# Expert weights in two transfers of 4 MB and two of 2 MB, with 32 KB and 16 KB of each partition in one run

## The reference

```python
h = h + mixed @ w_out[l]
h = h + moe(rms_norm(h, ffn_norm_w[l]), ...)
# moe:
logits = xt @ router_w + router_b
top_val, top_idx = lax.top_k(logits, 4)
gates = softmax(top_val)
# for each expert, on the tokens that chose it:
gu = xb @ w_gate_up[e] + b_gate_up[e]          # 1024 -> 2048
g, u = minimum(gu[:, :1024], 7), clip(gu[:, 1024:], -7, 7)
act = (u + 1) * (g * sigmoid(1.702 * g))
y = (act @ w_down[e] + b_down[e]) * gate       # 1024 -> 1024
```

## Time and profile before

| | |
|---|---|
| median of 3 runs | 1201.25 us (1198.61 to 1202.64) |
| profiled execution, first to last instruction (its span) | 1198.2 us; no other time of it was taken |
| TensorE busy | 1138.6 us (95%) |
| VectorE, ScalarE, GpSimd busy | 258.0, 172.6, 7.3 us |
| moved by DMA | 431.91 MB, mean 360 GB/s |
| gate/up loads | 256 of 1 MB, median 19.3 us from issue to landing |
| down loads | 128 of 1 MB, median 14.0 us |
| granted TensorE clock | 0.994 of full speed |

### The profile page before, as it was taken

How to read it: one execution, slowest core, us unless ns; L and a number is a source line. 1 busy time by engine, 2 the same in 40 slices (tenths; PEclk the granted TensorE clock), 3 DMA queues, 4 the chain that set the end, 5 groups by cost and what they waited for, 6 DMA issues and landing times.

```text
span 1198.2 us, 16109 instructions
## 1 busy us (share of the span) xinstructions
PE 1138.6 (95%) x6363; PEld 572.3 (48%) x6363; DVE 258.0 (22%) x657; ACT 172.6 (14%) x337; POOL 7.3 (1%) x16
## 2 busy tenths in 40 slices
PE   4999999799999999999999999999999999999997
PEld 3777776444444444444444444444444444444442
DVE  2487762631111111111111111111111111111101
ACT  2443240411000000000110000000000000000000
POOL 1000000000000000000000000000000000000000
PEclk9999999989999999999999999999999999999999
DMA  9953247699999959999999999999999999999995
GB/s 251 243 176 105 106 156 287 242 353 383 394 419 417 418 219 410 418 418 417 418 418 418 417 418 418 418 418 418 417 418 417 419 417 418 417 418 418 418 418 234
DMA packets 106452, 431.91 MB, mean 360 GB/s; under 512 B 9251, under 2 KB 37102, under 8 KB 73630
## 3 DMA queue, kind: packets, MB, share of 16 engines
q1 hardware_dynamic: 106206, 431.19, 90.8%
q0 software_dynamic: 224, 0.43, 0.1%
HBM read 430.54 MB, written 1.05 MB: 360 GB/s over the span
## 4 chain that ended last, share of the span: by engine, by line
PE 84%; DMA 7%; SPq 4%; ACT 3%; issue 1%; DVE 1%; DVEq 0%; ACTq 0%
PE psum L763 31%; PE psum L783 17%; PE psum L792 9%; DMA arena<-in_w_gate_up 6%; PE psum L566 5%; PE psum L750 4%; PE psum L732 4%; PE psum L486 4%; SPq L343 3%; PE psum L624 2%; PE psum L661 2%; ACT arena L999 1%; PE psum L592 1%; PE psum L742 1%; ACT arena L991 1%
## 5 line engine op out<-in xcount | busy, mean ns | idle before, releaser
L763 PE MATMUL psum<-arena 128*64 128x512 f32 x2048 | 448.4, 593 | 4.3 <-DMA arena<-in_w_gate_up 3.7
L763 PEld LDWEIGHTS psum<-arena 128*64 128x64 f32 x2048 | 192.2, 137 | 253.4 <-issue 240.0
L783 PE MATMUL psum<-arena 128*64 128x512 f32 x1024 | 228.3, 598 | 25.5 <-ACT arena L999 25.5
L1287 DVE TENSOR_SCALAR arena<-psum 128x512 f32<-128x512 f32 x32 | 22.1, 691 | 795.8 <-PE psum L763 784.0
L783 PEld LDWEIGHTS psum<-arena 128*64 128x64 f32 x1024 | 73.3, 138 | 159.9 <-issue 158.0
L792 PE MATMUL psum<-arena 128*128 128x512 f32 x256 | 117.8, 602 | 0.7 <-ACT arena L1003 0.7
L987 ACT COPY arena<-psum 128x512 f32<-128x512 f32 x32 | 18.7, 585 | 503.4 <-PE psum L732 503.4
L792 PEld LDWEIGHTS psum<-arena 128*128 128x128 f32 x256 | 45.8, 189 | 48.6 <-issue 47.0
L732 PEld LDWEIGHTS psum<-arena 128*128 128x128 bf16 x1536 | 48.4, 98 | 29.1 <-issue 29.1
L750 PE MATMUL psum<-arena 128*64 128x512 f32 x256 | 62.0, 598 | 0.0
L566 PE MATMUL psum<-arena 128*128 128x256 f32 x256 | 61.7, 385 | 0.3 <-ACT arena L924 0.3
(11 more groups left out here) (210 smaller groups left out, 540.6 us busy)
## 6 DMA issues: line engine op xcount, KB each, us to landing
arena<-in_w_gate_up SPq DMA_DIRECT2D x256, 1024.0 KB, 19.3
arena<-in_w_down SPq DMA_DIRECT2D x128, 1024.0 KB, 14.0
arena<-in_w_in SPq DMA_DIRECT2D x27, 512.0 KB, 6.7
arena<-in_w_out SPq DMA_DIRECT2D x1, 4096.0 KB, 16.8
arena<-in_w_o_mla SPq DMA_DIRECT2D x1, 2048.0 KB, 9.8
arena<-in_conv_pw_w SPq DMA_DIRECT2D x1, 2048.0 KB, 15.0
arena<-in_x SPq DMA_DIRECT2D x3, 512.0 KB, 6.5
out_y<-arena SPq DMA_DIRECT2D x4, 256.0 KB, 2.4
```

Of the source, the lines that this page charges most:

```text
L763: last = mm(b[64 * half:64 * half + 64, :], xe[i][:, k, :], gu[i][k][:, o + half * 512:o + half * 512 + 512], start=(k == 0 and bias_last) ...
L783: last = mm(Y[64 * c:64 * c + 64, :], aT[:, k % 4, 64 * (k // 4):64 * (k // 4) + 64], dn[i][:, u, c * 512:(c + 1) * 512], start=(k == 0), ...
```

## The change

- A gate/up load becomes two transfers of 4 MB. Partition p of half c gets rows 4p to 4p+3 of the half's 512 rows: 32 KB in one run. A down load becomes two of 2 MB, 16 KB a partition. There is one semaphore a transfer, and `gu_done` and `dn_done` count two an expert.
- As the rows of a weight block now belong to other partitions, the gathered state is stored in the matching order (`row_order`), and `turn_act` transposes every fourth column.
- `scatter` reads 64 partitions instead of 128; `wp` and `sT` shrink to two tiles, so `turn` has two transposes instead of four. The biases are kept at partitions 0 to 31 (gate) and 32 to 63 (up), and `pick` has 32 rows for each.
- The order of issue changes at EARLY = 20 instead of 6. The last expert's second down half is loaded in four pieces of 512 KB.
- Ahead of the items gu(0) waits for the ring as a whole, and gu(1) is loaded in two halves, after `h1_ready` and after `split_ready`.
- Clears of `biasgu` and `wp` on GpSimd go.

```diff
+GC, GR = 2, 4
+DC, DR = 2, 4
...
-        gu = [[words((A0, B0)[i] + 2048 * k, 2048) for k in range(KD)] for i in range(2)]
-        dn = [grid(D0 + 2048 * i, 2, 1024) for i in range(4)]
+        gu = [[grid((A0, B0)[i] + 8192 * c, GR, 2 * FF) for c in range(GC)] for i in range(2)]
+        dn = [grid(D0 + 4096 * h, DR, D) for h in range(DC)]
...
+        def row_order(y):
+            return y.rearrange("p (c q j) -> p c j q", c=GC, j=GR)
...
-                    src = weights_gu[e, k * P:(k + 1) * P, :]
...
-                sp.dma_start(gu[i][k], src).then_inc(in_gu[i][k], 16)
+                src = src[:, c * GR * P:(c + 1) * GR * P, :].rearrange("a (p j) f -> p (a j) f", j=GR)
+                sp.dma_start(gu[i][c], src).then_inc(in_gu[i][c], 16)
...
-                src = src[:, 2 * i * P:(2 * i + 2) * P, :].rearrange("a (k p) c -> p (a k) c", p=P)
-                sp.dma_start(dn[i], src).then_inc(in_dn[i], 16)
+                src = src[:, h * DR * P:(h + 1) * DR * P, :].rearrange("a (p j) f -> p (a j) f", j=DR)
+                sp.dma_start(dn[h], src).then_inc(in_dn[h], 16)
+
+            def load_last():
+                src = weights_dn[E - 1, DR * P:2 * DR * P, :].rearrange("(p j) f -> p j f", j=DR)
+                for j in range(DR):
+                    sp.dma_start(dn[1][:, j, :], src[:, j, :]).then_inc(in_last[j], 16)
...
-            for k in range(2, 6):
-                sp.wait_ge(*piece_used["g", k])
-                load_gu(0, 0, k)
+            sp.wait_ge(*piece_used["g", 7])
+            load_gu(0, 0, 0)
...
-            for k in (0, 1, 6, 7):
-                load_gu(0, 0, k)
+            load_gu(0, 0, 1)
             sp.wait_ge(S.mix_ready, 4)
...
+            sp.wait_ge(S.h1_ready, 4)
+            load_gu(1, 1, 1)
+            sp.wait_ge(S.hT_ready, 4)
             sp.wait_ge(S.xn_ready, 2)
+            sp.wait_ge(S.logits_ready, 2)
+            sp.wait_ge(S.split_ready, 2)
             load_gu(1, 1, 0)
...
-                for k in range(KD):
-                    sp.wait_ge(S.gu_done, 8 * (n - 2) + (k + 1))
-                    load_gu(n, u, k)
+                for c in range(GC):
+                    sp.wait_ge(S.gu_done, GC * (n - 2) + (c + 1))
+                    load_gu(n, u, c)
...
-                for i in range(4):
-                    sp.wait_ge(S.dn_done, 4 * (n - 1) + (i + 1))
-                    load_dn(n, i)
+                for h in range(DC):
+                    sp.wait_ge(S.dn_done, DC * (n - 1) + (h + 1))
+                    load_dn(n, h)
...
-            EARLY = 6
+            EARLY = 20
...
+            next_gu(E - 2, 0)
+            next_dn(E - 2)
+            next_gu(E - 1, 1)
+            sp.wait_ge(S.dn_done, DC * (E - 2) + 1)
+            load_dn(E - 1, 0)
+            sp.wait_ge(S.dn_done, DC * (E - 1))
+            load_last()
...
-                for c in range(2):
-                    for t in range(2):
-                        j = 2 * c + t
-                        last = nc.tensor.transpose(X[:, j * P:(j + 1) * P], wp[i][:, t, 64 - 64 * c:192 - 64 * c],
-                                                   ident)
+                for t in range(2):
+                    last = nc.tensor.transpose(X[:, t * P:(t + 1) * P], wp[i][:, t, :], ident)
...
-                        last = mm(b[64 * half:64 * half + 64, :], pick[i],
-                                  biasgu[:, o + half * 512:o + half * 512 + 512], start=first, stop=not first)
+                        last = mm(b[64 * half:64 * half + 64, :], pick[i][E * o:E * (o + 1), :],
+                                  biasgu[E * o:E * (o + 1), half * 512:half * 512 + 512], start=first, stop=not first)
...
-                        last = mm(total(t, c), sT[i][:, 2 * c + t, :], y_s, start=False, stop=False,
-                                  skip_group_check=True)
+                        last = mm(total(t, c), sT[i][64 * c:64 * c + 64, t, :], y_s[64 * c:64 * c + 64, :],
+                                  start=False, stop=False, skip_group_check=True)
...
-                for c in range(4):
-                    last = nc.tensor.transpose(Y[:, c * P:(c + 1) * P], a_s[:, c * P:(c + 1) * P], ident)
+                cols_of = a_s.rearrange("p (q j) -> p j q", j=DR)
+                for j in range(DR):
+                    last = nc.tensor.transpose(Y[:, j * P:(j + 1) * P], cols_of[:, j, :], ident)
```

More of the change, by code:

```diff
@@ L216, in layer @@
         xe = [grid(at + 1024 * i, KD, SLOTS) for i in range(2)]
-        sT = [grid(at + 1024 * i + 512, 4, P) for i in range(2)]
+        sT = [grid(at + 1024 * i + 512, 2, P) for i in range(2)]
         bdown = words(at + 1024, D); at += 2048
@@ L397, in _ @@
             next_dn(EARLY + 1)
-            with sp.Fori(0, (E - EARLY - 2) // 2) as it:
+            with sp.Fori(0, (E - EARLY - 4) // 2) as it:
                 for u in range(2):
@@ L407, in _ @@
                     e = sp.value_load(ove[0:1, bass.ds(j, 1)], min_val=0, max_val=E - 1)
[L408 to L413, removed]
+                    sp.wait_ge(S.gu_done, GC * j + GC * E)
+                    for c in range(GC):
+                        load_gu(e, 0, c)
+                    sp.wait_ge(S.dn_done, DC * j + DC * E)
+                    for h in range(DC):
+                        load_dn(e, h)
             for i in range(4):
@@ L758, in gate_up @@
                 pe.wait_ge(S.xe_ready, n + 1)
-                for k in range(KD):
-                    pe.wait_ge(in_gu[i][k], loads)
-                    for o, b in ((0, G), (FF, U)):
-                        for half in range(2):
-                            last = mm(b[64 * half:64 * half + 64, :], xe[i][:, k, :],
-                                      gu[i][k][:, o + half * 512:o + half * 512 + 512],
-                                      start=(k == 0 and bias_last), stop=(k == KD - 1 and not bias_last))
-                    if k == KD - 1 and bias_last:
+                for c in range(GC):
+                    pe.wait_ge(in_gu[i][c], loads)
+                    for j in range(GR):
+                        k = GR * c + j
+                        for o, b in ((0, G), (FF, U)):
+                            for half in range(2):
+                                last = mm(b[64 * half:64 * half + 64, :], xe[i][:, k, :],
+                                          gu[i][c][:, j, o + half * 512:o + half * 512 + 512],
+                                          start=(k == 0 and bias_last), stop=(k == KD - 1 and not bias_last))
+                    if c == GC - 1 and bias_last:
                         last = biases(i, False)
@@ L804, in item @@
                 turn_act(n)
-                down(n, dn_loads)
+                down(n, (dn_loads, dn_loads), in_pieces=final)
             free(6)
@@ L822, in _ @@
             turn_act(0)
-            down(0, 16)
+            down(0, (16, 16))
             gather(1, 1)
```

96 lines of the change are left out of this document (45 added, 51 removed).

## The result

The changed kernel takes 1171.9 us (median of 4 runs, 1167.8 to 1172.9). The kernel before, run beside it, takes 1201.5. The ratio is 0.975 (0.973 to 0.977), so 29.6 us are gone. The forecast was 1167, its range 1157 to 1194. The profiled execution took 1171.8 with a span of 1170.0, against a forecast span of 1163.6. The span is 6.4 us over its forecast and the time only 4.9: an execution takes 1.6 to 1.8 us more than its span, and the forecast had added 3.05.

What follows compares the result with a forecast made beforehand. The DMA weight stream was taken as the bound. Last landing: run length -26, switch -12, slower start +2, old hitches -2; the end gives back 4. Span 1163.6 plus 3.05 gave 1167 us, range 1157 to 1194.

Steps and rivals of the forecast that it cites:

- Runs: Weight stream: 96 fewer runs an engine and expert save 0.89 us, from 30.14 to 29.25 us an expert.
- B: Rival for the weight stream: it gets no faster, 30.14 us an expert, time 1193 us; chance 0.15.
- D: Rival for the weight stream: long runs read slower, kernel slower beyond 30.43 us an expert; chance 0.09.
- E: Rival: the same time, with a mildly slowed stream of 30.3 to 30.55 us an expert; chance 0.05.
- Scatter: TensorE's scatter in each item: from 3.52 to 1.76 us, perhaps 0.4 more, bounds 1.76 and 3.52.
- Biases: TensorE's biases in each item: unchanged at 1.72 us with 32 rows, lower bound below 0.9.
- The start of the stream: First loads: gu(3) issued at 285.1 flows from 287.4, 5 us unused; slower start +2 us.
- the permuted copies: Reordered copies of the state: cost nothing, as they lie beside the DMA bound.
- The gap at the switch: Change of issue order at dn(21): 0.8 us of transfer time unused instead of 13.0.
- The end: After gu(31) lands at 1136.5: 6.9 + 4.9 + 7.1 + 8.2 us to the span's end at 1163.6.
- the switch's 12 us: Moving the change of issue order from dn(7) to dn(21): -12 us of the last landing.

Runs made afterwards that it cites:

- the full scatter: Changed kernel with scatter over 128 rows and four transposes in turn again, biases still at 32 rows: 1177.74 us, ratio 0.9819.
- TensorE's part alone: Kernel before with scatter over 64 rows, two transposes in turn and biases with 32 rows; loads and order of issue unchanged: 1185.45 us, ratio 0.9872.
- run length alone undone: Changed kernel with each partition's rows 128 apart again, so runs of 8 KB (gate/up) and 4 KB (down), same transfers: 1195.55 us, ratio 0.9957.
- the half load ahead: Changed kernel with one half of gu(22) issued ahead of dn(21), the other behind its first half: 1169.01 us, ratio 0.9734.
- the finest version: Changed kernel with half of gu(22) ahead of dn(21), and gu(2), gu(3) first halves and gu(31) second half in 1 MB transfers: 1164.7 us, ratio 0.9697.

## Why the prediction was right, and what it missed

The mechanism held: the stream bounds the kernel, longer runs quicken it, and TensorE has to be out of its way. The profiled span came 6.4 us over the forecast, by terms that were mis-sized at the start and at the switch. Point by point:

**Runs: right, with some luck.** 29.25 us forecast, 29.22 measured. The rows were read as 7.5 to 9 ns a run, and the sum took 0.89 us, which is 9.3 ns a run, because eight completions would go as well. The completions cost nothing and a run costs 9.4 ns: two errors that cancel. With 7.5 ns the forecast would have been 29.42 us an expert and 5 us more in all. Rivals B (no faster), D (long runs slower) and E fall with this row. The pitch between partitions is the length of a run in each of the three layouts, so the two weren't tried apart; as all three lie on one line in the number of runs, a pitch of 32 KB did no harm that shows. The packets are 3,300 fewer than forecast because the small ones were not counted.

**Scatter: right.** 1.76 to 2.2 us forecast, 1.92 measured. By the Trainium skill ("TensorE: Matmul & The Clock Gate", Part 3) matmuls in different row groups run together; the trace agrees, 3.52 to 1.92 with the same eight instructions. Each of them takes as long as before, 615 ns in the mean against 602, but the two of a pair, one in the upper and one in the lower rows, start within 10 ns of each other. The end of the turn was then not late any more for the activation, as forecast.

**Biases: missed.** They stand at 1.72 in the sum, with the lower bound at 0.9; measured 1.02. The same mechanism as for scatter was assumed there and not carried over to here. So the item is 27.04 and not 27.8 us. It made no difference to the end, as the DMA was the bound either way, but the waits came at item 7 or 8 instead of about 10. Even with the full scatter it kept the item below the DMA's 29.2.

**The start of the stream: mis-sized, +3.7 us.** The forecast has gu(3) flowing from 287.4. Of the changed kernel, the first items of TensorE, then the issue of gu(3):

```profile
246.51 14.89 PE L772 MATMUL psum<-arena 128*64 128x512 f32 x64 [0.55 <-ACT arena L1029]
...
268.95 8.75 PE L795 MATMUL psum<-arena 128*64 128x512 f32 x32 [0.67 <-ACT arena L1013]
...
281.29 13.95 PE L772 MATMUL psum<-arena 128*64 128x512 f32 x64
```

```profile
L350 SPq DMA_DIRECT2D arena<-in_w_gate_up x1: 333/333/333, 288.6 to 288.6; - x1
...
DMA to landing us min/median/max: 12.2/12.2/12.2
```

It was issued at 288.6 and landed at 300.8. Its 4 MB take 9.72 at full rate, so it flowed from 291.1. The forecast built on TensorE's times of the earlier trace rows, and gate_up(0) began 3.06 us later. 1.8 of these are in the trace from the first matmuls on, which the change doesn't touch: 0.4 in 24 matmuls near 15 us (4.17 and 4.58 us) and most of the rest in the 96 behind them, first in the kernel before, then in the changed one:

```profile
19.84 22.16 PE L486 MATMUL psum<-arena 128*128 128x272 f32 x96 [0.39 <-DVE arena L1071]
```

```profile
20.16 23.62 PE L496 MATMUL psum<-arena 128*128 128x272 f32 x96 [0.38 <-DVE arena L1085]
```

The full clock was granted from 18.7 us in the one execution and from 23.2 in the other. In the profiles of the eight experiments it came between 18.8 and 19.5 or between 23.2 and 24.4 us, with no relation to their edits. A term read from a single profile carries this.

The other 1.3 us belong to the change. The forecast put the permuted copies at nothing, as lying beside the DMA bound. But the loads from gu(2) on wait for TensorE's first items, and these wait for the copies: a cast on ScalarE and a subtraction on VectorE stand ahead of the first gather (last line of each group); the kernel before, then the changed one:

```profile
233.11 1.04 ACT L974 CAST arena<-arena 128x1024 bf16<-128x1024 f32 x1 [1.55 <-DVE arena L1239]
234.69 1.22 DVE L1254 TENSOR_TENSOR arena<-arena 128x1024 f32<-128x1024 f32 x1
...
239.76 2.72 PE L732 MATMUL psum<-arena 128*128 128x64 bf16 x48 [3.87 <-DVE arena L1224]
```

```profile
234.91 2.00 ACT L987 CAST arena<-arena 128x1024 bf16<-128x1024 f32 x1 [1.55 <-DVE arena L1253]
236.95 1.96 DVE L1268 TENSOR_TENSOR arena<-arena 128x1024 f32<-128x1024 f32 x1 [0.36 <-ACT arena L987]
...
242.82 2.72 PE L742 MATMUL psum<-arena 128*128 128x64 bf16 x48 [5.12 <-DVE arena L1238]
```

With every fourth element of the normed state read, they took 2.00 and 1.96 us instead of 1.04 and 1.22, and the wait grew from 3.87 to 5.12. In the run with 8 and 4 KB, which copies in plain order, they took 1.04 and 1.22 again and the wait was 3.93; with elements in neighbouring pairs (the runs of 16 KB) they took 1.10 and 1.22, and it was 3.96.

**The gap at the switch: mis-sized, 3.6 instead of 0.8 us.** TensorE did wait for dn(20), and dn(21) went out 3.7 us behind the landing, as the forecast has it. TensorE at that place, then SyncE's longest wait, the issue of dn(20)'s second half, and the issue of dn(21)'s first and second half, all in the changed kernel:

```profile
842.70 3.65 PE L795 MATMUL psum<-arena 128*64 128x512 f32 x16 [1.47 <-DMA arena<-in_w_down]
```

```profile
SPq L356 <- PE psum L795: 57.3, 5, 23.7
...
L356 SPq DMA_DIRECT2D arena<-in_w_down x1: 333/333/333, 822.2 to 822.2; - x1
...
DMA to landing us min/median/max: 25.3/25.3/25.3
...
L356 SPq DMA_DIRECT2D arena<-in_w_down x2: 338/340/343, 846.4 to 851.3; - x2
...
DMA to landing us min/median/max: 7.8/8.7/9.7
```

dn(20)'s second half landed at 847.5, and dn(21) at 854.2 and 860.9: 6.7 and 6.7 apart, where 4.89 is the distance in a full stream. So the gap is 2 x 1.8 = 3.6. The first 1.8 are explained. A lone transfer of 2 MB took 7.8 us, 2.9 more than its 4.89 in a full stream, and the forecast took 2.25, read from transfers of 1 MB in the earlier trace rows: 846.4 + 2.9 - 847.5 = 1.8. The forecast ended its count there. But dn(21)'s second half needs the second half of down(20), which ran until 851.2, and so its first bytes were due at 851.3 + 2.9 = 854.2, the very moment of the first half's landing, with no lead. Why it came another 1.8 late, and not just in time, stays open.

**A hitch, +1.0 us, not in the sum.** gu(3)'s second half landed 10.7 us behind the first, where 9.72 is the distance in a full stream; why is open. The stream's pace gives 0.3 back.

**The end: right.** TensorE's last items in the changed kernel, and its last transfers, for the earlier trace rows:

```profile
1143.69 7.09 PE L772 MATMUL psum<-arena 128*64 128x512 f32 x32 [0.26 <-DMA arena<-in_w_gate_up]
1150.71 1.99 PE L805 MATMUL psum<-arena 64*128 64x512 f32 x8
...
1155.12 7.09 PE L795 MATMUL psum<-arena 128*64 128x512 f32 x32 [0.68 <-ACT arena L1013]
1162.89 1.99 PE L805 MATMUL psum<-arena 64*128 64x512 f32 x8 [0.69 <-ACT arena L1017]
...
L362 SPq DMA_DIRECT2D arena<-in_w_down x4: 328/432/434, 1135.4 to 1136.7; - x4
```

gu(31) landed at 1143.6 instead of 1136.5, 7.1 late; the terms above (start, gap, hitch, pace) are 3.7 + 2.8 + 1.0 - 0.3 = 7.2. From there to the span's end are 26.4 us, where 6.9 + 4.9 + 7.1 + 8.2 = 27.1 were forecast. So 1163.6 + 7.1 - 0.7 = 1170.0. The last byte came even later, at 1154.9 (1136.7 + 18.1, 1146.3 forecast), but the half that it belongs to is read only in the second half of down, from 1158.7 on.

**The sum of the parts.** TensorE's part alone gave 16.4 us. Long runs gave 23.7. From "TensorE's part alone" (1185.45) to "run length alone undone" (1195.55) the run lengths are the same, and what differs is the transfers of 4 and 2 MB with their order at the start, at the switch and at the end: they cost 10.1. The balance is -16.4 + 10.1 - 23.7 = -30.0. That it meets the -29.6 measured directly proves nothing, as the four kernels are a chain from the one before to the changed one and the middle ones drop out of the sum. Of the 10.1, the finer transfers and the half load ahead got back 7.2. The forecast had the size of the whole nearly right, but gave the switch's 12 us to the order of issue. The runs give them to the faster item: with it and the old order the changed kernel took the same 1171.9 us, while the new order without it was worth 6.

**Still open.** What decides when the first full clock is granted was not found, nor what delays the second transfer behind an empty queue. How the 7.2 us of the finest version divide was not tried apart; its profile puts 0.6 at the end. Nor was scatter tried with 64 rows that stay in one half of the array.

## What to carry to other kernels

When a kernel streams weights at the DMA's limit, count the contiguous runs per engine and price them from two layouts in the trace: bytes and 9.4 ns a run give the pace of three layouts. A reading from two transfer sizes of one trace gives the order of the price only, 7.5 to 9 ns here. Ask also what the new layout costs where the activations have to be put in its order. Large transfers give nothing for their size beyond their longer runs, and they are dear wherever the queue is empty or the work behind it starts with a landing, so keep the long runs in the steady stream and cut the transfers finely at the first loads, at a change of order and at the last one (which gave 0.6 us here). When an idle stretch of the DMA starts with a wait for a buffer, look at the engine that frees it before changing the order.

## What the runs showed of the hardware

- Matmuls with 64 rows that alternate between the halves of the array ran at 0.24 us each instead of 0.44 (1.92 / 8, 3.52 / 8), in float32; those with 32 rows, which also alternate between the halves of the columns as before, at 0.13 instead of 0.22 (1.02 / 8, 1.72 / 8).
- A contiguous run costs one DMA engine 9.4 ns beside its bytes, the same between 4 to 8 KB and 16 KB as between 16 and 32 KB. The number of transfers in a full stream, four or twelve an expert, made no difference (30.12 us with four; 30.14 and 30.12 with twelve).
- Behind a wait of 1.96 us for a DMA the granted clock was at the lower level for a part of the next group of matmuls, which took 8.78 us instead of 7.09. It cost nothing of the kernel's pace where the DMA bounds it (30.91 + 27.52 = 2 x 29.22).
- The first full clock came at 18.7 to 24.4 us in different executions; 18.7 against 23.2 moved TensorE by 1.8 us.
- A float32 cast of 1024 elements a partition on ScalarE took 2.00 us with every fourth element read and 1.04 in plain order, a subtraction on VectorE with one operand read so 1.96 instead of 1.22; with neighbouring pairs 1.10 and 1.22.
